# Moving the small matrix products of a projection part from between its two token tiles to behind the second one

## What is computed

```python
def hybrid_layer(x, ...):
    h = rms_norm_2(x, n_pre_mix)
    proj = h @ w_in
    (u_pool, g_q, g_k, g_v, g_r, g_a1, m_cq, m_ckv, m_kr, gate_logits) = jnp.split(proj, IN_OFFSETS, axis=-1)
    y_a = pool_mixer(u_pool, w_pool, pool_scale) @ w_a
    y_b = gla_mixer(g_q, g_k, g_v, g_r, g_a1, w_gla_a2, b_gla_a, gla_norm) @ w_b
    y_c = mla_mixer(m_cq, m_ckv, m_kr, cos, sin, mla_q_norm, w_mla_uq, mla_kv_norm, w_mla_ukv) @ w_c
    gates = jax.nn.sigmoid(gate_logits...).reshape(b, s, N_BRANCH, d)
    merged = gates[:, :, 0] * y_a + gates[:, :, 1] * y_b + gates[:, :, 2] * y_c
    x = x + rms_norm_2(merged @ w_o, n_post_mix)
    h = rms_norm_2(x, n_pre_ffn)
    gu = h @ w_ffn_gu
    ffn = (jax.nn.silu(gu[..., :D_FF_2]) * gu[..., D_FF_2:]) @ w_ffn_down
    return x + rms_norm_2(ffn, n_post_ffn)
```

## Time and profile before

| | us |
|---|---|
| median of 3 timed executions | 1899.73 (1899.44 to 1900.01) |
| the profiled execution's own time | 1899.96 |
| its span, first to last instruction | 1897.8 |
| PE busy | 1884.5 (99%) |
| weight loads on PE | 1639.1 (86%) |
| DVE busy | 1340.7 (71%) |
| ACT busy | 967.5 (51%) |
| POOL busy | 161.5 (9%) |
| mean granted TensorE clock | 0.998 of full |

### The profile page before, as it was taken

The page is one execution under the profiler, slowest core; times in us unless marked ns, Lnnn a source line. Parts: engine busy times, 40 slices in busy tenths (PEclk is TensorE's granted clock), DMA queues, the critical chain, the costliest instruction groups (busy, mean ns, idle before and its releaser), DMA issues.

```text
span 1897.8 us, 26159 instructions
## 1 busy us (share of the span) xinstructions
PE 1884.5 (99%) x10937; PEld 1639.1 (86%) x10940; DVE 1340.7 (71%) x1485; ACT 967.5 (51%) x1216; POOL 161.5 (9%) x158
## 2 busy tenths in 40 slices
PE   9999999999999999999999999999999999999998
PEld 7888879888888888898888888888888888888887
DVE  7877687787687777868776555569765654568764
ACT  5444656544444446665434665455444665455442
POOL 0000522100000006121000200000000110000000
PEclk9999999999999999999999999999999999999999
DMA  7554543455555555334554443445545343445452
GB/s 289 205 185 177 189 153 104 150 200 184 187 196 186 189 182 178 134 112 178 192 190 167 165 171 133 164 169 189 188 173 187 136 174 135 158 178 180 186 176 112
DMA packets 47491, 327.28 MB, mean 172 GB/s; under 512 B 5520, under 2 KB 5520, under 8 KB 11536
## 3 DMA queue, kind: packets, MB, share of 16 engines
q1 hardware_dynamic: 46512, 323.25, 47.0%
q10 hardware_dynamic: 864, 2.38, 0.3%
HBM read 324.56 MB, written 1.05 MB: 172 GB/s over the span
## 4 chain that ended last, share of the span: by engine, by line
PE 97%; DVE 1%; ACT 1%; issue 0%; DMA 0%; POOL 0%; DVEq 0%; POOLq 0%; ACTq 0%
PE ps L537 34%; PE ps L544 18%; PE ps L525 10%; PE ps L527 10%; PE ps L526 10%; PE ps L865 2%; PE ps L531 1%; PE ps L831 1%; PE ps L820 1%; PE ps L822 1%; PE ps L821 1%; PE ps L854 1%; PE ps L582 1%; PE ps L532 1%; PE ps L741 1%
## 5 line engine op out<-in xcount | busy, mean ns | idle before, releaser
L331 ACT CAST w_hi<-raw 128x2048 fp32r<-128x2048 f32 (+4 forms) x314 | 580.1, 1849 | 574.0 <-PE ps L527 193.7
L338 DVE TENSOR_TENSOR w_lo<-raw,w_hi 128x2048 fp32r<-128x2048 f32 (+4 forms) x314 | 700.1, 2231 | 237.8 <-ACT w_hi L331 235.1
L537 PE MATMUL ps<-x_hl,w_hi 128*128 128x512 f32 x1968 | 459.3, 390 | 0.0
L537 PEld LDWEIGHTS ps<-x_hl,w_hi 128*128 128x128 f32 x1968 | 365.2, 188 | 73.2
L525 PE MATMUL ps<-w_hi,x_hl 128*128 128x512 f32 (+3 forms) x672 | 262.5, 391 | 0.0
L527 PE MATMUL ps<-w_hi,x_hl 128*128 128x512 f32 (+3 forms) x672 | 254.3, 378 | 0.0
L526 PE MATMUL ps<-w_lo,x_hl 128*128 128x512 f32 (+3 forms) x672 | 253.6, 377 | 0.0
L544 PEld LDWEIGHTS ps<-x_hl,w_lo 128*128 128x128 f32 x1968 | 243.6, 192 | 5.5 <-DVE w_lo L338 1.4
L544 PE MATMUL ps<-x_hl,w_lo 128*128 128x256 f32 x1968 | 246.8, 283 | 0.8 <-DVE w_lo L338 0.8
L1816 DVE TENSOR_REDUCE ffn_tmp<-ps 128x512 f32<-128x1024 f32 x132 | 161.2, 1223 | 100.3 <-PE ps L544 50.2
L537 PE MATMUL ps<-hid_hl,w_hi 128*128 128x512 f32 x836 | 196.4, 390 | 0.0
(11 more groups left out here) (288 smaller groups left out, 2204.3 us busy)
## 6 DMA issues: line engine op xcount, KB each, us to landing
raw<-in_parts SPq DMA_DIRECT2D x278, 1024.0 KB, 4.8
raw<-in_parts SPq DMA_DIRECT2D x20, 768.0 KB, 4.2
raw<-in_parts SPq DMA_DIRECT2D x4, 928.0 KB, 4.5
raw<-in_parts SPq DMA_DIRECT2D x4, 864.0 KB, 4.4
raw<-in_parts SPq DMA_DIRECT2D x6, 512.0 KB, 3.7
raw<-in_parts SPq DMA_DIRECT2D x4, 576.0 KB, 3.6
const<-in_const ACTq DMA_DIRECT2D x1, 1093.0 KB, 5.1
h<-in_x_t SPq DMA_DIRECT2D x1, 1024.0 KB, 7.6
```

The costliest lines, as they stand in the source:

```text
L331: nc.scalar.copy(w_hi[:, i % RING, 0:n_of(i)], raw[:, i % RING, 0:n_of(i)]).then_inc(high_ready, 1)
L338: nc.vector.tensor_tensor(w_lo[:, s, 0:n], raw[:, s, 0:n], w_hi[:, s, 0:n].bitcast(F32), ALU.subtract).then_inc(low_ready, 1)
L537: m = nc.tensor.matmul(ps[:, bank, :], w_h(c), hl(c).rearrange("p x n -> p (x n)"), start=start and c == 0, stop=stop and c == kc - 1, ski ...
```

## The change

`project` still takes a `between` argument, but `mixer2` no longer gives it one; `within_part(m)` is called after the whole part, right before `after_part(m)`. No instruction is added, removed or altered, no wait is added or removed, and the orders of ACT, DVE, POOL and SP are as before. In the first block's mixer nothing moves.

```diff
@@ -1186,7 +1186,8 @@
                     if g == 0 and CHUNKWISE[s]:
                         project_by_chunk(i0 + m, pair_bank(g), kc, o, k == 0, last, ready)
                     else:
-                        project(i0 + m, pair_bank(g), kc, o, k == 0, last, free, ready, x, lambda: within_part(m))
+                        project(i0 + m, pair_bank(g), kc, o, k == 0, last, free, ready, x)
+                    within_part(m)
                     after_part(m)
```

## The result

The changed kernel takes **1905.34 us** (median of 6 executions, 1904.07 to 1907.42) against 1899.51 for the kernel before in the same session (6 executions, 1899.38 to 1900.01): a ratio of 1.0031, 95% interval 1.0021 to 1.004. It is slower by 5.8 us, inside the range and 0.04 us from the predicted time. The agreement is better than the reasoning behind it: the six executions lie in two groups, 1904.07 to 1904.56 and 1906.12 to 1907.42, and the median falls in the empty space between.

A forecast was written before the change was run, and what follows sets the result against it. PE was taken to bound the kernel, with 97% of the chain. Terms 2.34 + 2.28 + 1.68 - 0.56 - 0.20 = +5.5 us on 1899.96 gave 1905.5, stated as 1905.3 for the median; range 1902.7 to 1907.2.

The forecast's parts named there:

- Second mixer, m = 2: Sums-to-turn chain through POOL and ACT, where PE already waits 0.29: sums and turn come one tile later, +2.34 us.
- First mixer, m = 1: Sums move to the end of m = 1; all of m = 2 still covers the trip, 0.39 us spare: cost 0.
- m = 13: Both mixers, first head turns: PE waits for ACT's squares and copies, m = 14 begins 1.14 us later in each.
- m = 19: Both mixers, last turn of probabilities: the weighing waits for ACT's copy, +0.84 us each, taken as upper bound.
- m = 16 to 18: Scores of the next batch stand between turn and weighing and hide ACT's copies: cost 0.
- m = 7: Both mixers: part 5 ends ahead of the gate logits, ACT frees the banks earlier, PE's wait of 0.28 us goes.
- Fewer breaks: m = 4, 14, 16, 17, 18 of each mixer: moved pieces join others, 0.02 us saved at each, -0.20 in all.
- The clock's rival: Second mixer, m = 2: PE's clock falls to 1.2 GHz in the new 2.6 us wait, +1.65, 1906.9 us; chance 0.14.
- POOL's root: Second mixer, m = 2: rival that the root takes 2.34 us instead of 0.70, +1.64, 1906.9 us; chance 0.05.
- the dearest break: Rival that fifteen removed breaks cost more than counted: at 0.28 us each, +1.5, 1901.2 us; chance 0.16.

The follow-up runs named there:

- the kernel with the rest moved: Against the kernel before, all pieces moved behind the second tile except m = 13, m = 19 and the second mixer's sums at m = 2: 1898.14 us, -1.4.

## Why the prediction was right, and where it was not

The number is right and so are the mechanisms of its sum, but its closeness is luck: two errors cancel in it.

- **Second mixer, m = 2: +2.34.** Measured +2.36, the wait 2.58 for a predicted 2.6, released by the line that was named. Right.
- **First mixer, m = 1: 0.** Right; no wait at the turn, and in the kernel with the rest moved nothing is lost there.
- **m = 13: 1.14 in each mixer.** Measured 1.12 and 1.14 alone, 1.15 in the change. Right, and so is its working: the copies come late by ACT's two squares. Of the two waits foretold, PE shows one.
- **m = 19: 0.84 in each.** Measured 0.83 alone; the upper bound was the right one to take, since ACT began 1.08 behind the turn though it had been idle for 1.20.
- **m = 16 to 18: 0.** No wait there. Right.
- **m = 7: -0.28 in each.** The mechanism was right, the size off: -0.44. I counted the gap, and neither the slow restart behind it (0.08) nor the small delays around it (0.08).
- **Fewer breaks (changes between large and small products): -0.02 at each place, -0.10 in each mixer.** Mis-sized: -0.25 in each. I priced only the late restart behind a small piece (0.09) and set against it a base of -0.07 read from four and eight transposes; the start of the piece is late as well, by 0.06, and at m = 17 a whole break came to 0.17. That is more than the bound of 0.09 a place and than the 0.1 by which I had said the sum would be wrong; over all places it stayed inside the bounds.
- Together the sum without the clock was +5.5 and is +4.95 to +5.0.
- **The clock's rival, chance 0.14.** This is the step that failed. By their times it happened in 8 of 14 executions of the changed kernel, and in up to 11 of 11 of the kernel with the sums alone moved. Its price, 1.65, was good: 1.5 for the usual 3.4 us (9 products at 0.36 instead of 0.195 are 1.5), 2.7 for the long stretch. My argument against it, that PE had been at 2.4 GHz for a millisecond and so would not fall, did not hold: with the wait filled, and nothing else changed, the clock stayed up in both traces, and no execution was as slow as those with a fall. So it is the idleness in those 2.6 us that lets the clock fall, though not in every execution. The better evidence was in the earlier trace rows, a fall right behind a wait of 2.11. The Trainium skill, TensorE: Matmul & The Clock Gate, section "Why this matters for your kernels", warns of idle gaps between bursts of matmuls, but of somewhat longer ones than this. Here the measurement decides: 2.58 us were enough in four of six traces.
- POOL's root stayed at 0.70, and the dearest break was 0.17 where 0.38 each would have turned the sign: both rivals are out.

So 0.5 too much in the sum and a clock that I left out of it made 5.5, between the two groups at +5.0 and +6.5. Had I taken the clock for the likeliest case, the same sum would have given 1906.9, 1.6 above the median: the right case with a sum still 0.5 too high.

## What to carry to other kernels

A small product whose result goes out to another engine and comes back should be issued ahead of the tile that can hide the trip: each such place cost what the tile had hidden of the trip (2.36, 1.14, 0.83). Places with other work behind the turn, or where no one waits, cost nothing and even gained 0.25 in a mixer by fewer changes between large and small products. With the small piece behind it, a part also ends earlier for the engines that wait for its end, which can pay: at m = 5 it let ACT free a bank in time. And a new idle stretch of PE, here 2.58 us, has two prices, its length and, in some executions, half the clock for a while; filling it with work that nobody reads took 1.5 us back and did not lengthen the wait. Of the versions tried, the one that moves all but m = 13, m = 19 and the second mixer's sums was the fastest, 1.4 us under the kernel before, which is little more than the executions differ by.

## What the runs showed of the hardware

The same wait of PE, 2.58 us in six traces, was followed by a fall to 1.2 GHz in four and by none in two. In the four the clock fell at different moments: once inside the wait (0.9 before PE started again), and three times after PE had restarted, by 0.3 to 1.4 us, with products running at full speed until then. The low stretch was 3.4 us three times and 6.8 us in the one where it began inside the wait. The length of the wait alone thus doesn't decide; what does is open.

Nor is it shown that the kernel with the sums alone moved had the fall in every execution. One of its eleven, at 1903.90, has a mean granted clock of 1.000, where 3.4 us at half speed would leave 0.999 at most. Its time is like the others', so there it has another reason, which stays open.

At the program's start PE's first wait for ACT differs by the execution. PE restarts at 7.14 to 7.46, but the ten products ahead of the wait end at 5.01 to 5.76, depending on when the clock rises. Three traces, of the kernel with all but three places moved, of the changed kernel's second trace and of its first:

```profile
7.43 4.02 PE L582 MATMUL ps<-unsel 128*128 128x512 bf16 x10 [2.42 <-ACT w_hi L315]
```

```profile
7.40 2.33 PE L582 MATMUL ps<-unsel 128*128 128x512 bf16 x10 [1.91 <-ACT w_hi L315]
```

```profile
7.14 3.75 PE L582 MATMUL ps<-unsel 128*128 128x512 bf16 x10 [1.38 <-ACT w_hi L315]
```

Behind the first the granted clock fell to 0.50, behind the second it stayed at 1.00, and the ten products took 2.33. In the third they took 3.75. They were 0.43 apart until 10.08, as the products ahead of the wait were, and 0.22 from there on: the clock had not yet risen when the wait began, so this trace can't show a fall. (Its windows print a granted clock of 1.00 there, since the clock's record begins only with the rise.) Over all 14 traces the clock fell behind waits of 2.0, 2.1 (four times) and 2.4. It stayed up behind 1.5, 1.6 (twice), 1.7 and 1.9, and had not yet risen in the three with 1.4, 1.5 and 1.6. So the length does sort the eleven that can tell. But it is not shown to be the cause: in the six with a fall the clock had also risen earliest, at 4.1 to 4.9, against 5.1 to 6.5 in the five without, and an earlier rise makes the wait longer.
